# Products of split weights that read the moving tile from the last token to the first, and write the accumulator in the same order

## The chip, the core and the metric

The kernel runs on one core of one Trainium2 chip. The metric is the device time of one launch in microseconds. A core has five instruction streams that matter here: TensorE (PE, with its weight loads listed as PEld), VectorE (DVE), ScalarE (ACT), GpSimd (POOL) and the DMA queues, of which SyncE (SP) issues the weight loads from memory.

## The reference: what is computed

Two blocks of a language model run one after the other over 512 tokens of width 1024, all in float32. The first block projects the normalised input with one matrix `w_in` into four groups of heads (softmax attention with a forget gate, a gated delta rule, two gated linear attentions), projects the result back with `w_out`, and then runs a feed-forward layer with a short convolution (`w_up`, `w_down`, inner width 2816). The second block is a convolution mixer (`conv_w_in`, `conv_w_out`) with a gated feed-forward layer, then latent attention (`w_dkv`, `w_dq`, `w_ukv`, `w_uq`, `w_o`) with another feed-forward layer and a final norm. Cut to what matters here:

```
x = x + token_mix(rms_norm(x), w_in) @ w_out
x = x + conv_glu_ffn(rms_norm(x), w_up, w_down)
h = h + short_conv_mixer(rms_norm_2(h), conv_w_in, conv_w_out)
h = h + swiglu_ffn(rms_norm_2(h), w13, w2)
h = h + mla_mixer(rms_norm_2(h), w_dq, w_uq, w_o, shared_kv(h))
h = h + swiglu_ffn(rms_norm_2(h), w13, w2)
```

Nearly all arithmetic is in the products with the weight matrices. Each has all 512 tokens on one side.

## The kernel before, in words

Activations are kept transposed: features on the 128 partitions, the 512 tokens along the free axis, one tile for each 128 features (`xT`, eight tiles). Weights come in **units**: 128 output columns of a matrix with up to eight blocks of 128 input rows. SP loads a unit into one of four `raw` buffers. ACT copies it into `whi` with rounding to the format fp32r (line 358), and DVE subtracts to get the remainder `wlo` (line 366). There are two `whi` and two `wlo` buffers. Activations are split in the same way into a high and a low tile (`xhi`, `xlo`; `h_hi`, `h_lo` for feed-forward products; `c_hi`, `c_lo` and `chi`, `clo`, `lhi`, `llo` elsewhere).

The function `product` multiplies one unit with the 512 tokens. For each block of input rows it calls `passes`, which issues three matmuls into the same accumulator: high weight with high activation (line 371), high with low (372), low with high (373). The weight is the stationary side (128 x 128), the activation tile the moving side (128 x 512, fp32r), and the output is one whole PSUM bank (128 x 512, float32). `acc(tile)` alternates between two banks. With eight blocks, a unit is a chain of 24 matmuls that add into one bank. The last of the chain carries the semaphore increment (`unit_used` or a named step) that its readers wait for: the evacuation by DVE or ACT out of the bank (line 621 in the up-projections, line 543 in the residuals), and the split of a later unit, which needs the freed `whi` and `wlo`. No reader looks at part of a bank before the chain has ended.

One more place calls `passes` directly (line 2004): the values of the latent attention, where the activation is the stationary side and the weight unit the moving one. The kernel's other matmuls (transposes, the delta rule's triangles and chunks, attention scores) are float32 and do not go through `passes`.

The order of the work on each engine is written out by hand, with hardware loops for the repeated units. PE starts a product when its unit's low half is ready and the bank has been read.

Of the kernel before, what the change touches and what calls it, by code (L numbers as in the profile page):

```python
# [180 lines left out]
class Steps:  # L181
# [8 lines left out]
    def step(self, engine, name):  # L190
        assert name not in self.at, name
        self.count[engine] += 1
        self.at[name] = (engine, self.count[engine])
        return self.sems[engine], 1
# [43 lines left out]
def build(nc, A, cst_d, out_d, known):  # L238
    ctx = ExitStack()
    with ctx:  # L240
# [25 lines left out]
        def acc(tile):  # L266
            return ps[:, tile % 2, :]
# [46 lines left out]
        def unit_view(buf, u):  # L314
            _, kt, n, _ = UNITS[u]
            return buf[:, u % (RAW if buf is raw else PARTS), 0:kt * n].rearrange("p (k c) -> p k c", c=n)
# [4 lines left out]
        def in_loop(value, i, per):  # L321
            return value if i is None else value + per * i
# [46 lines left out]
        def passes(out, wh, wl, xh, xl, first, last):  # L369

            t_.matmul(out, wh, xh, start=first, stop=False)  # L371
            t_.matmul(out, wh, xl, start=False, stop=False)  # L372
            return t_.matmul(out, wl, xh, start=False, stop=last)  # L373

        def product(pe, u, tile, i=None, per=0, x=(xhi, xlo), k0=0, start=True, stop=True, ready=None, cols=0,
                    full=None, order=None, ks=None, reads=False):


            kt = UNITS[u][1]
            pe.wait_ge(lo_split, in_loop(u + 1, i, per))  # L380
            for n, k in list(enumerate(order or range(kt)))[slice(*(ks or (0, kt)))]:
                if ready is not None:
                    ready(pe, k0 + k)
                wh, wl = (unit_view(b, u)[:, k, cols:cols + P] for b in (whi, wlo))
                last = passes(acc(tile), wh, wl, x[0][:, k0 + k, :], x[1][:, k0 + k, :],
                              start and n == 0, stop and n == kt - 1)
                if reads and n < kt - 1:
                    last.then_inc(x_read, 1)
            if ks is None or ks[1] == kt:
                last.then_inc(*(step("pe", full) if full else (unit_used, 1)))  # L390
# [86 lines left out]
        def pe_residual(pe, stage, thirds, x, ready, order=None):  # L477

            per, np_, tiles = round_of(thirds)
            parts = THIRDS if thirds else ((0, KT),)  # L480
            n0 = TILE0[stage]
            regained = x[0] is xhi

            def body(i, last, begin=0):
                for j in range(begin, per):
                    m, part = divmod(j, np_)
                    reads = last and j == per - 1
                    if part == 0:
                        pe.wait_ge(acc_free, n0 + m + 1 + tiles * i)
                    product(pe, FIRST[stage] + j, m, i, per, x, parts[part][0], part == 0, part == np_ - 1,  # L490
                            ready if m == 0 else None, order=None if reads else order, reads=reads)
            if x[0] is c_hi:
                for m, ks in ((0, (0, KT - 1)), (1, (0, KT // 2)), (0, (KT - 1, KT)), (1, (KT // 2, KT))):
                    if ks[0] == 0:
                        pe.wait_ge(acc_free, n0 + m + 1)
                    product(pe, FIRST[stage] + m, m, x=x, ready=ready if m == 0 else None, ks=ks)
                body(0, False, 2)
            with pe.Fori(x[0] is c_hi, KT // tiles - regained) as i:
                body(i, False)
            if regained:  # L500
                body(KT // tiles - 1, True)
# [70 lines left out]
        def pe_up(pe, stage, name, gain, residual):  # L572
            n0 = TILE0[stage]

            def body(i, first):
                for j in range(4):
                    pe.wait_ge(acc_free, n0 + j + 1 + 4 * i)
                    product(pe, FIRST[stage] + j, j, i, 4, ready=parts_of(gain) if first and j == 0 else None)
                    if first and j == 0:
                        pe_sum(pe, name, NORM0[residual])  # L580
            body(0, True)
            with pe.Fori(1, FT // 2) as i:
                body(i, False)
# [2014 lines left out]
```

## Time and profile before

| | |
|---|---|
| median of two runs | 1940.74 us (1940.49 to 1941.0) |
| span of the profiled execution | 1938.3 us |
| median less span | 2.4 us |
| PE busy | 1890.5 us, 98% of the span, 9271 matmul records |
| PEld, DVE, ACT, POOL busy | 1540.8, 959.2, 739.5, 237.1 us |
| mean granted TensorE clock | 0.986 of full speed |
| memory traffic | 161 MB, 83 GB/s |

The span is the time from the first to the last instruction that the hardware profiler recorded in one execution. It has no separately measured time of its own beside it; the span with the 2.4 us by which the median exceeds it is what the sums in this document are made against. Matmuls overlap in the records: one lasts 389 ns by its record while the next has started after some 226 ns. So the sum of durations is more than the busy time, and what a matmul costs in a chain is read from one start to the next. A float32 matmul of the program leaves two records, an fp32r matmul one.

### The profile page before, as it was taken

What the parts mean: (1) busy time and instruction counts of PE and PEld (TensorE: products, weight loads), DVE (VectorE), ACT (ScalarE), POOL (GpSimd) and SP (SyncE); (2) the same over time, 40 slices, a digit from 0 to 9 for tenths busy, and PEclk for the clock granted to TensorE, in tenths of its full rate; (3) what the DMA queues carried; (4) which work ended last, traced back from release to release, by engine and by line L of the source; (5) the groups of instructions that cost most, each with busy time, mean ns of one, the idle gap of its engine ahead of it and who ended that gap; (6) DMA issues with size and microseconds to landing.
All of it is one profiled execution on the core that took longest, in us unless ns stands there. A gap on an engine that the chain in (4) does not pass through costs nothing.

```text
span 1938.3 us, 25963 instructions
## 1 busy us (share of the span) xinstructions
PE 1890.5 (98%) x9271; PEld 1540.8 (79%) x9271; DVE 959.2 (49%) x1354; ACT 739.5 (38%) x1075; POOL 237.1 (12%) x196
## 2 busy tenths in 40 slices
PE   8989999999999999999999999999999999999998
PEld 6778867667888888888888888888776778888887
DVE  6464466654777763344454444333647444444322
ACT  6542543554444443232253333232455343333222
POOL 0051000102111111000021111101000121111100
PEclk9999998999999999999999999999999999999999
DMA  6310211113333333333333333333320133333332
GB/s 193 87 33 1 55 34 34 34 47 89 103 97 97 94 94 94 98 98 98 98 88 104 94 95 97 92 99 101 92 83 22 44 95 94 94 96 96 100 90 73
DMA packets 309223, 161.34 MB, mean 83 GB/s; under 512 B 12688, under 2 KB 306832, under 8 KB 309024
## 3 DMA queue, kind: packets, MB, share of 16 engines
q1 hardware_dynamic: 308080, 157.67, 28.1%
q0 software_dynamic: 640, 2.17, 0.3%
q8 instruction: 48, 0.79, 0.2%
q10 hardware_dynamic: 432, 0.52, 0.1%
q14 instruction: 23, 0.19, 0.0%
HBM read 158.24 MB, written 2.10 MB: 83 GB/s over the span
## 4 chain that ended last, share of the span: by engine, by line
PE 91%; DVE 4%; ACT 3%; issue 1%; POOL 0%; DMA 0%; ACTq 0%; DVEq 0%; POOLq 0%
PE ps L371 26%; PE ps L372 26%; PE ps L373 26%; PE ps L1063 1%; PE ps L1743 1%; PE ps L1491 1%; PE ps L1075 1%; PE ps L1501 1%; PE ps L2039 1%; PE ps L2040 1%; PE ps L1734 1%; PE ps L936 1%; ACT whi L358 1%; PE ps L920 1%; PE ps L1455 0%
## 5 line engine op out<-in xcount | busy, mean ns | idle before, releaser
L371 PE MATMUL ps<-xhi,whi 128*128 128x512 f32 x1656 | 656.6, 396 | 3.1 <-ACT ecol L989 2.1
L372 PE MATMUL ps<-xlo,whi 128*128 128x512 f32 x1656 | 647.7, 391 | 0.0
L373 PE MATMUL ps<-xhi,wlo 128*128 128x512 f32 x1656 | 647.6, 391 | 0.0
L358 ACT ACTIVATE whi<-raw 128x1024 fp32r<-128x1024 f32 (+2 forms) x297 | 309.0, 1040 | 707.6 <-PE ps L373 707.0
L366 DVE TENSOR_TENSOR wlo<-raw,whi 128x1024 fp32r<-128x1024 f32 (+2 forms) x297 | 365.8, 1232 | 278.6 <-ACT whi L358 278.6
L371 PEld LDWEIGHTS ps<-xhi,whi 128*128 128x128 f32 x1656 | 313.1, 189 | 72.1 <-issue 7.9
L373 PEld LDWEIGHTS ps<-xhi,wlo 128*128 128x128 f32 x1656 | 312.8, 189 | 65.9
L372 PEld LDWEIGHTS ps<-xlo,whi 128*128 128x128 f32 x1656 | 313.1, 189 | 65.3 <-issue 2.2
L621 DVE TENSOR_TENSOR zS<-ps,rs 128x512 f32<-128x512 f32 x132 | 91.3, 692 | 296.8 <-PE ps L373 284.6
L373 PE MATMUL ps<-h_hi,wlo 128*128 128x512 f32 x528 | 205.4, 389 | 0.0
L371 PE MATMUL ps<-h_hi,whi 128*128 128x512 f32 x528 | 205.4, 389 | 0.0
L372 PE MATMUL ps<-h_lo,whi 128*128 128x512 f32 x528 | 205.4, 389 | 0.0
L646 POOL TENSOR_TENSOR h_lo<-xg,h_hi 128x512 f32 x66 | 84.9, 1286 | 639.8 <-ACT h_hi L607 639.8
L562 POOL TENSOR_TENSOR ssq<-ssq,sq 128x512 f32<-128x512 f32 x48 | 78.6, 1638 | 555.9 <-ACT sq L510 555.9
L372 PEld LDWEIGHTS ps<-h_lo,whi 128*128 128x128 f32 x528 | 99.1, 188 | 20.7
L373 PEld LDWEIGHTS ps<-h_hi,wlo 128*128 128x128 f32 x528 | 99.1, 188 | 20.6
L371 PEld LDWEIGHTS ps<-h_hi,whi 128*128 128x128 f32 x528 | 99.1, 188 | 20.4
L607 ACT ACTIVATE h_hi<-xg 128x512 f32 x66 | 41.7, 632 | 144.7 <-DVE xg L637 144.7
L543 DVE TENSOR_TENSOR xT<-ps,xT 128x512 f32<-128x512 f32 (+1 forms) x48 | 33.2, 691 | 119.9 <-PE ps L373 119.9
L445 DVE SCALAR_TENSOR_TENSOR xlo<-xT,pcol,xhi 128x512 fp32r<-128x512 f32 (+1 forms) x48 | 47.1, 1009 | 12.6 <-ACT xhi L439 12.6
L439 ACT ACTIVATE xhi<-xT,pcol 128x512 fp32r<-128x512 f32 (+1 forms) x48 | 32.8, 717 | 4.4 <-DVE xT L543 1.0
L510 ACT ACTIVATE sq<-xT 128x512 f32<-128x512 f32 (+1 forms) x48 | 30.1, 626 | 11.1 <-DVE xT L543 10.3
(339 smaller groups left out, 1718.7 us busy)
## 6 DMA issues: line engine op xcount, KB each, us to landing
raw<-in_conv_ffn_w SPq DMA_DIRECT2D x52, 512.0 KB, 3.8
raw<-in_mla_ffn_w SPq DMA_DIRECT2D x52, 512.0 KB, 3.8
raw<-in_w_up SPq DMA_DIRECT2D x44, 512.0 KB, 3.8
raw<-in_w_in SPq DMA_DIRECT2D x28, 512.0 KB, 3.8
raw<-in_conv_w_in SPq DMA_DIRECT2D x24, 512.0 KB, 3.7
raw<-in_w_down SPq DMA_DIRECT2D x16, 448.0 KB, 3.5
raw<-in_conv_ffn_w SPq DMA_DIRECT2D x16, 448.0 KB, 3.5
raw<-in_mla_ffn_w SPq DMA_DIRECT2D x16, 448.0 KB, 3.4
```

The lines of the kernel that those rows point to most:

```text
L358: a.activation(whi[:, u % PARTS, 0:n], raw[:, u % RAW, 0:n], ACT.Copy).then_inc(hi_split, 1)
L366: e.tensor_tensor(wlo[:, u % PARTS, 0:n], raw[:, u % RAW, 0:n], f32(whi[:, u % PARTS, 0:n]), ALU.subtract).then_inc(lo_split, 1)
L371: t_.matmul(out, wh, xh, start=first, stop=False)
L372: t_.matmul(out, wh, xl, start=False, stop=False)
L373: return t_.matmul(out, wl, xh, start=False, stop=last)
L439: a.activation(tile_of(xT if name == "final_norm_g_2" else xhi, k), tile_of(xT, k), ACT.Copy, scale=gain_of(name, k)).then_inc(x_hi, 1)
L445: v.scalar_tensor_tensor(tile_of(xlo, k), tile_of(xT, k), gain_of(name, k), f32(tile_of(xhi, k)), ALU.mult, ALU.subtract).then_inc(x_lo, 1)
L543: v.tensor_tensor(x, acc(m), x, ALU.add).then_inc(acc_free, 1)
L562: g.tensor_tensor(ssq[:, :], ssq[:, :], sq[:, m, :], ALU.add).then_inc(summed, 1)
L607: a.activation(tile_of(h_hi, m), xg[:, pair, :], ACT.Copy).then_inc(prod_hi, 1)
L621: v.tensor_tensor(z, acc(j), rs[:, :], ALU.mult).then_inc(acc_free, 1)
L646: g.tensor_tensor(tile_of(h_lo, m + 2 * i), xg[:, m, :], f32(tile_of(h_hi, m + 2 * i)), ALU.subtract).then_inc(prod_lo, 1)
```

## The change

`product` hands `passes` the accumulator and both activation tiles with the free axis turned round: the first column that is streamed is token 511, the last is token 0, and column by column the output goes to the same token's place as before. The stationary side (`wh`, `wl`), the order of the matmuls, the semaphores, the buffers and everything on other engines are as they were. On every engine the order of the instructions is the same in both kernels (4042 on PE as written, loops not unrolled). The call of `passes` at line 2004 is not changed.

```
--- before.py
+++ after.py
@@ -382,7 +382,7 @@
                 if ready is not None:
                     ready(pe, k0 + k)
                 wh, wl = (unit_view(b, u)[:, k, cols:cols + P] for b in (whi, wlo))
-                last = passes(acc(tile), wh, wl, x[0][:, k0 + k, :], x[1][:, k0 + k, :],
+                last = passes(acc(tile)[:, ::-1], wh, wl, x[0][:, k0 + k, ::-1], x[1][:, k0 + k, ::-1],
                               start and n == 0, stop and n == kt - 1)
                 if reads and n < kt - 1:
                     last.then_inc(x_read, 1)
```

## Rows read from the trace of the kernel before

**Rows 1.** The page: busy time by engine, then the chain of waits.
```profile
PE 1890.5 (98%) x9271; PEld 1540.8 (79%) x9271; DVE 959.2 (49%) x1354; ACT 739.5 (38%) x1075; POOL 237.1 (12%) x196
PE 91%; DVE 4%; ACT 3%; issue 1%; POOL 0%; DMA 0%; ACTq 0%; DVEq 0%; POOLq 0%
```

**Rows 2.** Groups by shape on PE: line, out<-moving,stationary, count | busy us, mean ns | idle before.
```profile
L371 PE MATMUL ps<-xhi,whi 128*128 128x512 f32 x1656 | 656.6, 396 | 3.1 <-ACT ecol L989 2.1 <-DVE xlo L829 1.0
L371 PE MATMUL ps<-h_hi,whi 128*128 128x512 f32 x528 | 205.4, 389 | 0.0
L371 PE MATMUL ps<-c_hi,whi 128*128 128x512 f32 x64 | 24.9, 390 | 0.0
L371 PE MATMUL ps<-chi,whi 128*128 128x512 f32 x36 | 14.9, 415 | 0.3 <-ACT qp L2088 0.3
L371 PE MATMUL ps<-lhi,whi 128*128 128x512 f32 x16 | 7.0, 440 | 0.0
L371 PE MATMUL ps<-whi,lhi 128*128 128x512 f32 x16 | 6.4, 401 | 1.4 <-ACT vtok L2075 1.4
```

**Rows 3.** Busy time by stretch (us from the start): records in brackets, then PE's clock.
```profile
300.00:400.00 100.00, 92.87 (x691) 69.17 (x690) 65.46 (x137) 49.08 (x85) 13.75 (x12) 0.89 0.15 48
600.00:700.00 100.00, 100.00 (x443) 82.81 (x442) 70.06 (x83) 41.59 (x54) 11.62 (x9) 1.00 0.33 97
700.00:800.00 100.00, 100.00 (x443) 82.81 (x442) 40.72 (x41) 31.19 (x37) 10.35 (x8) 1.00 0.32 94
1700.00:1800.00 100.00, 100.00 (x443) 82.83 (x442) 40.18 (x46) 30.12 (x37) 12.43 (x10) 1.00 0.33 96
```

**Rows 4.** PE in order of time, in an up-projection: start us, duration us.
```profile
700.08 0.39 PE L371 MATMUL ps<-xhi,whi 128*128 128x512 f32 x1
700.30 0.39 PE L372 MATMUL ps<-xlo,whi 128*128 128x512 f32 x1
700.53 0.39 PE L373 MATMUL ps<-xhi,wlo 128*128 128x512 f32 x1
700.76 0.39 PE L371 MATMUL ps<-xhi,whi 128*128 128x512 f32 x1
```

**Rows 5.** Who waited for the last matmul of a chain (line 373): us, times.
```profile
  ACT whi L358: 707.0, 219
  DVE zS L621: 284.6, 127
  DVE xT L543: 119.9, 45
```

**Rows 6.** PE in order of time, attention scores in float32 (two records each).
```profile
1459.35 1.02 PE L2039 MATMUL ps<-kn,qn 128*128 128x512 f32 x2
1460.21 1.02 PE L2040 MATMUL ps<-kpz,qp 128*128 128x512 f32 x2
1461.49 0.30 PE L1734 MATMUL ps<-cst,mla_P 128*128 128x128 f32 x1 [0.26 <-DVE mla_P L1794]
```

**Rows 7.** PE in order of time: line 1075, moving runs of 2, then of 32.
```profile
131.93 3.69 PE L1075 MATMUL ps<-mx 128*128 128x64 f32 x32
...
167.32 3.68 PE L1075 MATMUL ps<-mx 128*128 128x64 f32 x32
```

**Rows 8.** Groups on DVE by shape: a scan forward (1517), a scan backward (1519).
```profile
L1517 DVE TENSOR_TENSOR_SCAN mx<-mx 128x512 f32<-128x512 f32 x3 | 3.6, 1216 | 0.0
L1519 DVE TENSOR_TENSOR_SCAN mx<-mx,lastone 128x512 f32<-128x512 f32 x3 | 3.6, 1197 | 0.0
```

More of the change, by code:

```diff
@@ L384, in product @@
                 wh, wl = (unit_view(b, u)[:, k, cols:cols + P] for b in (whi, wlo))
-                last = passes(acc(tile), wh, wl, x[0][:, k0 + k, :], x[1][:, k0 + k, :],
+                last = passes(acc(tile)[:, ::-1], wh, wl, x[0][:, k0 + k, ::-1], x[1][:, k0 + k, ::-1],
                               start and n == 0, stop and n == kt - 1)
```

## The prediction

> **What bounds the kernel now.** I read the page's first part and its chain of waits first. PE is busy for 1890.5 us of 1938.3 and holds 91% of the chain; DVE, at 959.2 us, is the next engine and has half of that [rows 1]. So the time is PE's, and the question is which of PE's work the change touches. The groups by shape say that [rows 2]: line 371 ran 1656 + 528 + 64 + 36 + 16 = 2300 times with an activation tile as the moving side, and lines 372 and 373 as often, which makes 6900 matmuls that get a reversed moving tile and a reversed output. The last row of the group, 16 of each line with `whi` moving, is the direct call of `passes` and stays as it was: 48 matmuls.
>
> What one of them costs is not its duration (389 ns) but the distance between starts. The windows show 443 records in each 100 us of three stretches that hold nothing but products, with the clock at 1.00 (the upper of the two levels, 2.4 GHz) and PE busy 100.00 us: 100/443 = 225.7 ns for one [rows 3]. The timeline shows the same from near: 700.08 to 700.76 for three, 227 ns each, with no gap at line 373, the end of a triple [rows 4]. So the products take 6900 x 0.2257 = 1557 us, 80% of the span. The other 381 us are float32 matmuls and stages where DVE and ACT are waited for; there the clock falls too (0.89 between 300 and 400 us) [rows 3].
>
> The readers of a bank wait for the chain's last matmul and for nothing before it: 707.0 us of ACT's idle time and 284.6 and 119.9 us of DVE's end there [rows 5]. That idle time is slack of engines off the path. It also says that the direction in which a bank is filled is seen by no reader: when the last matmul ends, all of the bank is there, in either direction.
>
> **The change part by part.**
>
> Instructions: none is added, taken away or moved, on any engine. The cost of issue and of the semaphores is 0. No wait goes and none comes, so nothing is late next as long as a matmul takes as long as before. If one took longer, PE would still be the bound, since DVE is idle for half of the time and the DMA engines are busy for a third (0.33) [rows 1, 3].
>
> The one term is therefore 6900 x d, where d is what the reversed direction adds to the 225.7 ns of one product matmul. No matmul of the kernel before has a negative step, on the moving side or on the output, so d is bounded by the nearest rows.
>
> The upper bound is the rate at which this kernel's float32 matmuls take 512 columns. Two records of line 2039 start at 1459.35 and line 2040 follows at 1460.21, so one record, a stream of 512 columns, takes 430 ns [rows 6]. That is what a product costs if a column needs a whole slot for itself in place of sharing one with its neighbour: d = 430 - 225.7 = 204.3 ns, or 6900 x 0.2043 = 1410 us.
>
> The lower bound comes from the same rows. Half of 430 is 215, so the product's 225.7 has 10.7 ns in it beyond the column stream at twice that rate. If something in the seam between two matmuls of a chain costs those 10.7 ns and the reversed order avoided it, d = -10.7 ns and the term is -74 us.
>
> What row is nearest? Two bear on it. VectorE has a scan over 512 elements that reads and writes with step -1, in float32, just behind a forward one of the same shape: 1197 ns against 1216, so reading and writing SBUF backwards costs this engine nothing [rows 8]. It is another engine and at 2.3 ns an element a much slower one, so it says little about a stream at 0.44 ns a column. On PE itself, line 1075 reads its moving side in runs of 2 columns (every other pair) at 131.93 and in runs of 32 at 167.32: 3.69 and 3.68 us for 32 records, 115 ns a record in both [rows 7]. Broken runs of moving columns cost nothing that shows. This is weaker than it looks, because 64 columns at 430/512 ns are 54 ns, and so anything up to twice that is hidden in the 115 ns.
>
> I take d = 0. The streamed columns have the same addresses and the same neighbours in memory as before, and so have the output columns; only the order within a pair turns. The distance between two additions to one column stays 512 columns, since all matmuls of a chain run the same way. The seams between a reversed chain and a forward matmul are few (a chain of 24 runs between them), and even at 10.7 ns for each of some 297 units they are 3 us.
>
> The row on runs of two [rows 7] reads the moving side only; its output is written straight on. On the output the Trainium skill has a rule against this change: its page "Advanced Engine Details and Errata", section "Memory Cachelines", says that PSUM works in lines of two float32 values and that every two consecutive elements should be contiguous, or matmuls slow down significantly. If a falling step counts as not contiguous, the page leads to the half-rate case below; if what counts is that both columns lie in one line, it leads to my forecast. No run so far shows which.
>
> The sum: span 1938.3 + 6900 x 0 = 1938.3 us, and with the 2.4 us by which the median lies above the span, 1941 us, the median of before.
>
> **The rivals.**
>
> *Half rate.* Each pair of columns is no longer taken together, on the way in from SBUF or on the way out to PSUM, and a product matmul takes as long as a float32 record, 430 ns. The place is every product chain; the cost is +1410 us, so 3350 us. It decides as soon as the pairing works for rising addresses alone, and a tenth of its price would already be 141 us. Stages where PE waits now could take up at most its idle time, 1938.3 - 1890.5 = 48 us, so between 3300 and 3350 us. For it speaks that a product gets its 512 float32-wide columns through at 512/225.7 = 2.27 columns a nanosecond, nearly twice the rate of the float32 records [rows 4, 6]: something there handles more than one column at a time, and such a thing may have a direction. Against it speaks that a backward stream costs VectorE nothing [rows 8].
>
> *A dearer seam.* The stream keeps its rate, but each reversed matmul starts with the upper end of a line and pays once more what the seam costs now, 10.7 ns. 6900 x 10.7 ns = +74 us: 2015 us, slower by 3.8%. It needs only 5.6 ns a matmul (39 us in all) to pass 2%. Rows 4 show that matmul follows matmul without any slack for it.
>
> *A cheaper seam.* The 10.7 ns are lost between two matmuls in a way that depends on the direction, and go: 1941 - 74 = 1867 us. The Trainium skill's page "TensorE: Matmul & The Clock Gate", section "Back-to-back issue gap", gives N/2.4 + 2.5 ns, 216 ns for 512 columns, where this trace has 225.7; it says nothing of a direction. What stands against this is that nothing in the trace ties the extra time to the order of the columns; the records of the weight load (442 in 100 us, 82.8 us busy) are as good a candidate, and they don't change [rows 3].
>
> *The change does nothing at all*, because the direction is lost on the way to the chip, gives the forecast's number too.
>
> **How the numbers follow.** The forecast with d = 0 (and the direction that is lost) gets 0.68: one scan and one pattern of short runs, both clean, and no consumer that could see the difference. Half rate gets 0.18: its mechanism is plain, and the product's 0.44 ns a column is a rate that no backward row of the trace has been seen at. The dearer seam gets 0.11, the cheaper 0.03. The time is the likeliest one, 1941 us. By itself the forecast would lie within 1936 to 1946. The range has to hold 8 in 10, so it takes in the dearer seam at the top, 2015 us; on the low side the cheaper seam is too unlikely to be needed, and 1935 closes the range, which holds 0.68 + 0.11 = 0.79, with small seam gains in it about 0.8. The half rate stays outside. About 2% is what a measurement of this kernel can tell from no change, and that gives: faster 0.03, within 2% 0.69 (a seam dearer by under 5.6 ns is in it), slower 0.28.
>
> **What would show it.** In the profile after, the stretch from 700 to 800 us should again hold 443 records at clock 1.00 and three matmuls of a unit should start 0.23 us apart with durations of 389 ns. Busy times of DVE, ACT and POOL should be the same to a microsecond or two. With half rate the window would hold some 232 records, line 371's mean would rise from 389 to about 590 ns, and the idle time of ACT and DVE behind line 373 would about double. With the dearer seam there would be 423 records. If the time rose with the windows at 443, the cause would lie in the other 381 us, which I hold untouched; if the rise differed between chains with `xhi` and with `h_hi` as the moving tile, it would lie in the buffers' places and not in the direction.

## The result, and the profile after

The changed kernel takes 1983.75 us in the median (1983.6 to 1983.9) against 1940.74 before: a ratio of 1.0231, with a 95% interval from 1.0192 to 1.027. It is slower by 43 us. That it is slower is clear; that it is slower by more than 2% is not, from these two executions on each side. The time lies in the stated range. The likeliest case, no change, did not come. What came has the form of the rival named "a dearer seam", a fixed addition to each matmul, at 58% of its price.

The page of the changed kernel, busy time by engine and then the chain of waits, answers to [rows 1]:

```profile
PE 1935.9 (98%) x9271; PEld 1546.2 (78%) x9271; DVE 953.8 (48%) x1354; ACT 740.6 (37%) x1075; POOL 235.9 (12%) x196
PE 92%; DVE 4%; ACT 2%; issue 1%; POOL 0%; DMA 0%; ACTq 0%; DVEq 0%; POOLq 0%
```

PE is busy 45.4 us longer (1935.9 against 1890.5), with the same number of records; the span grew by 43.5 us (1981.8 against 1938.3). So all of it lies in PE's own work, and PE's waits even shrank by 2 us. Nothing else moved by more than 6 us.

The windows of the changed kernel (records in brackets, the clock in the third column from the right) answer to [rows 3]:

```profile
600.00:700.00 100.00, 100.00 (x431) 80.71 (x430) 66.96 (x81) 41.68 (x54) 11.53 (x9) 1.00 0.32 94
700.00:800.00 100.00, 100.00 (x430) 80.77 (x429) 42.94 (x46) 32.15 (x39) 10.13 (x8) 1.00 0.31 92
1700.00:1800.00 100.00, 100.00 (x430) 80.72 (x430) 39.92 (x45) 29.45 (x36) 11.49 (x9) 1.00 0.31 92
```

There are 430 to 431 records where 443 stood, at the same clock and with PE as full as before. Such a count takes in the one or two records that began before the window, so dividing 100 us by it gives a distance that is about 1 ns too short. Starts that lie far apart give the distance itself. These are starts of line 371, first one of the kernel before, then two of the changed kernel:

```profile
500.16 0.39 PE L371 MATMUL ps<-xhi,whi 128*128 128x512 f32 x1
```

```profile
500.45 0.40 PE L371 MATMUL ps<-xhi,whi 128*128 128x512 f32 x1
699.96 0.40 PE L371 MATMUL ps<-xhi,whi 128*128 128x512 f32 x1
```

In the kernel before, 294 triples (a triple is the three matmuls of one call of `passes`) lie between 500.16 and 700.08 us [rows 4]: 680.0 ns a triple, 226.7 ns a matmul. In the changed kernel 285 triples lie between the two starts: 700.0 and 233.3 ns. That is 6.7 ns more for each product matmul, and 6900 x 6.7 ns = 46 us. It accounts for PE's 45.4 us.

The profile holds a control inside the same run. These are rows of line 373 of the changed kernel, durations in ns as smallest, median, largest:

```profile
L373 PE MATMUL ps<-h_hi,wlo x528: 397/398/398, 722.8 to 1968.9; 128*128 128x512 f32 x176
L373 PE MATMUL ps<-c_hi,wlo x64: 397/398/398, 981.3 to 1025.4; 128*128 128x512 f32 x64
L373 PE MATMUL ps<-chi,wlo x36: 395/398/398, 1460.2 to 1488.6; 128*128 128x512 f32 x36
L373 PE MATMUL ps<-lhi,wlo x16: 397/398/399, 1433.6 to 1446.7; 128*128 128x512 f32 x16
L373 PE MATMUL ps<-whi,llo x16: 388/389/390, 1447.4 to 1459.5; 128*128 128x512 f32 x16
```

Each of these buffers that is read backward shows 398 ns in the median, where it had 389 before, and with hardly any spread. The last row is the direct call of `passes`, which still reads forward: it stayed at 389, between neighbours in time that did not (`lhi`, until 1446.7 us, and `chi`, from 1460.2 us). So the cost follows the direction, and neither the buffer nor the stage. The recorded duration rose by 9 ns and the distance between starts by 6.7; since matmuls overlap in the records, the distance is what counts.

### The profile page after: what moved, and what is told of

It reads as the page before. It is cut to its first block, busy times and chain, and to the rows that moved or that the text cites. A ratio compares the mean times of both kernels' runs of the same rounds, so it can differ in the third digit from the quotient of the medians.

```text
span 1981.8 us, 25963 instructions
## 1 busy us (share of the span) xinstructions
PE 1935.9 (98%) x9271; PEld 1546.2 (78%) x9271; DVE 953.8 (48%) x1354; ACT 740.6 (37%) x1075; POOL 235.9 (12%) x196
## 4 chain that ended last, share of the span: by engine, by line
PE 92%; DVE 4%; ACT 2%; issue 1%; POOL 0%; DMA 0%; ACTq 0%; DVEq 0%; POOLq 0%
PE ps L371 27%; PE ps L373 27%; PE ps L372 27%; PE ps L1063 1%; PE ps L1743 1%; PE ps L1491 1%; PE ps L1075 1%; PE ps L2039 1%; PE ps L2040 1%; PE ps L1501 1%; PE ps L1734 1%; PE ps L920 1%; PE ps L936 1%; PE ps L1455 1%; DVE xlo L445 0%
## 5 line engine op out<-in xcount | busy, mean ns | idle before, releaser
L371 PE MATMUL ps<-xhi,whi 128*128 128x512 f32 x1656 | 670.9, 405 | 3.2 <-DVE wlo L366 2.1
L372 PE MATMUL ps<-xlo,whi 128*128 128x512 f32 x1656 | 662.3, 400 | 0.0
L373 PE MATMUL ps<-xhi,wlo 128*128 128x512 f32 x1656 | 661.8, 400 | 0.0
L358 ACT ACTIVATE whi<-raw 128x1024 fp32r<-128x1024 f32 (+2 forms) x297 | 308.8, 1040 | 745.3 <-PE ps L373 743.7
L366 DVE TENSOR_TENSOR wlo<-raw,whi 128x1024 fp32r<-128x1024 f32 (+2 forms) x297 | 360.7, 1215 | 286.7 <-ACT whi L358 286.6
L621 DVE TENSOR_TENSOR zS<-ps,rs 128x512 f32<-128x512 f32 x132 | 91.3, 692 | 321.2 <-PE ps L373 308.9
L373 PE MATMUL ps<-h_hi,wlo 128*128 128x512 f32 x528 | 210.0, 398 | 0.0
L371 PE MATMUL ps<-h_hi,whi 128*128 128x512 f32 x528 | 209.9, 398 | 0.0
L372 PE MATMUL ps<-h_lo,whi 128*128 128x512 f32 x528 | 209.9, 398 | 0.0
```

The source lines that it names most:

```text
L358: a.activation(whi[:, u % PARTS, 0:n], raw[:, u % RAW, 0:n], ACT.Copy).then_inc(hi_split, 1)
L366: e.tensor_tensor(wlo[:, u % PARTS, 0:n], raw[:, u % RAW, 0:n], f32(whi[:, u % PARTS, 0:n]), ALU.subtract).then_inc(lo_split, 1)
L621: v.tensor_tensor(z, acc(j), rs[:, :], ALU.mult).then_inc(acc_free, 1)
```

## The experiments

Two questions were open. The first is the side: theory R puts the cost where the moving tile is read, theory W where the accumulator is written. The second is the form: for either side, the cost can be fixed for each matmul (theory F, the seam) or gather by the column or by the step down (theory L). Twelve kernels were run, the first two timed in three rounds, the rest with one profile each. In the profiles I read the number of records in 100 us of pure products, as above, and where single nanoseconds matter the distance of starts between 500 and 700 us. The kernel before took between 1935.3 us (mean clock 0.990) and 1942.3 us (0.985) in 13 executions beside the one-sided kernels, so a difference of under 7 us between two single executions says nothing by itself.

### One side alone

```
-                last = passes(acc(tile), wh, wl, x[0][:, k0 + k, :], x[1][:, k0 + k, :],
+                last = passes(acc(tile), wh, wl, x[0][:, k0 + k, ::-1], x[1][:, k0 + k, ::-1],
```

> Only the moving side of the products runs backward; the output is written forward, so each accumulator holds its tokens in the wrong order and the result is not the reference's. Theory R (the extra time arises where the moving tile is read from SBUF): 1984 us, 430 records in 100 us of a product stretch, as with both reversed. Theory W (it arises where the accumulator is written): 1941 us, 443 records. If both sides contribute: between the two, and the other one-sided kernel has the rest.

```
-                last = passes(acc(tile), wh, wl, x[0][:, k0 + k, :], x[1][:, k0 + k, :],
+                last = passes(acc(tile)[:, ::-1], wh, wl, x[0][:, k0 + k, :], x[1][:, k0 + k, :],
```

> Only the output of the products runs backward; the moving side is read forward, so the tokens stand in the wrong order and the result is not the reference's. Theory W (writing the accumulator backward costs the time): 1984 us, 430 records in 100 us. Theory R (reading backward costs it): 1941 us, 443 records.

Moving side alone: 1984.05 us, ratio 1.0232 (1.0215 to 1.0249) to the kernel before on the same chip. Output alone: 1940.03 us, ratio 0.9994 (0.9983 to 1.0006). The windows agree; first the kernel that reads backward, then the one that writes backward:

```profile
600.00:700.00 100.00, 100.00 (x430) 80.59 (x429) 67.36 (x81) 42.05 (x54) 11.54 (x9) 1.00 0.32 93
700.00:800.00 100.00, 100.00 (x431) 80.55 (x430) 42.63 (x45) 31.76 (x39) 10.14 (x8) 1.00 0.32 92
```

```profile
600.00:700.00 100.00, 100.00 (x443) 82.84 (x442) 71.13 (x83) 42.12 (x55) 11.95 (x10) 1.00 0.32 94
700.00:800.00 100.00, 100.00 (x443) 82.84 (x442) 41.14 (x42) 31.19 (x37) 10.34 (x8) 1.00 0.33 97
```

This settles the side. All of the cost is in reading the moving tile; writing float32 columns to PSUM in falling order costs nothing, to within two tenths of a per cent (0.9983 to 1.0006). Theory W is out, and with it, for a falling step, the Trainium skill's rule of the page "Advanced Engine Details and Errata", section "Memory Cachelines", that I had weighed against the change: adjacent columns in falling order were as good as in rising order here.

### One matmul of three backward

```
-            t_.matmul(out, wh, xl, start=False, stop=False)
+            t_.matmul(out[:, ::-1], wh, xl[:, ::-1], start=False, stop=False)
```

> Of the three matmuls of a triple only the middle one runs backward, moving side and output both; the other two forward. If the cost belongs to each reversed matmul (6.3 ns by 43 us / 6900): a third of it, 1955 us, some 439 records in 100 us. If it belongs to a chain in which every matmul starts at the upper end, or to the turn from one direction to the other: 1941 us in the first case; in the second, two turns in each triple, well over 1955 us, since the column written last is then the one that the next matmul adds to first.

It took 1954.96 us, 439 records in 100 us. The groups by shape of this kernel (mean ns behind the busy time) show where:

```profile
L372 PE MATMUL ps<-h_lo,whi 128*128 128x512 f32 x528 | 209.1, 396 | 0.0
L373 PE MATMUL ps<-h_hi,wlo 128*128 128x512 f32 x528 | 205.9, 390 | 0.0
L371 PE MATMUL ps<-h_hi,whi 128*128 128x512 f32 x528 | 205.4, 389 | 0.0
```

By their starts, three matmuls take 686.7 ns against 680.0 before: 6.7 ns more for one backward matmul among forward ones, a third of the change's 20 ns. The cost belongs to the backward matmul itself (line 372, 396 ns), and a turn of direction between two matmuls adds nothing, though the next one then adds first to the column that was written last. The edit also turned the middle matmul of the direct call, 16 in all, which is 0.1 us.

### How fine must the falling order be?

In these four kernels both sides go down in blocks and forward within a block; the block has b columns.

```
+        def down(ap):
+
+            return ap.rearrange("p (n b) -> p n b", b=2)[:, ::-1, :]
...
-                last = passes(acc(tile), wh, wl, x[0][:, k0 + k, :], x[1][:, k0 + k, :],
+                last = passes(down(acc(tile)), wh, wl, down(x[0][:, k0 + k, :]), down(x[1][:, k0 + k, :]),
```

With b = 2:

> Both sides run through pairs of columns: the last pair first, within a pair forward (steps -2 and 1). If the falling order inside a pair is what costs: 1941 us. If going down from line to line or starting at the top costs: 1984 us. If a pattern of two dimensions has a price of its own or breaks the pairing: more than 1984 us.

With b = 4:

> As the run with pairs, but in blocks of four columns (16 bytes of a partition): the last block first, within a block forward, on both sides. If the cost comes from leaving or entering a 16-byte line at the wrong end: 1941 us. If it comes from going down through memory at all, or from starting near the top of the tile: 1984 us.

With b = 256:

> Both sides run forward in two blocks of 256 columns, the upper block first: one step down in each matmul. If any step down costs a fixed time: 1984 us. If starting away from the tile's first column costs it: 1984 us too. If the cost gathers over many small steps down, or lies in a start that is not on a larger boundary: 1941 us.

With b = 16:

> Both sides in blocks of 16 columns, the last block first, within a block forward: 31 steps down in a matmul, where blocks of four have 127 and the full cost. Theory F (a fixed cost of a matmul that goes down, whatever the number of steps): 1984 us, 430 records in 100 us. Theory L (each step down costs a little, 6.5 ns / 127): 6900 x 1.6 ns = 11 us more than before, 1952 us, 440 records.

With b = 64:

> The same in blocks of 64 columns: 7 steps down. Theory F: 1984 us, 430 records. Theory L: 6900 x 0.36 ns = 2.5 us more, 1943 us, 442 to 443 records. If the cost is only there when the first step down comes within some number of columns from the start: 1941 us here and 1984 us with 16, or 1941 us with both.

| block | steps down | us | records, 600 to 700 us |
|---|---|---|---|
| 1 (the change) | 511 | 1983.75 | 431 |
| 2 | 255 | 1983.07 | 430 |
| 4 | 127 | 1985.5 | 431 |
| 16 | 31 | 1983.8 | 431 |
| 64 | 7 | 1938.41 | 443 |
| 256 | 1 | 1942.15 | 443 |
| 512 (before) | 0 | 1940.74 | 443 |

The windows of the kernels with blocks of 16 and of 64, in that order:

```profile
600.00:700.00 100.00, 100.00 (x431) 80.55 (x430) 67.28 (x81) 41.86 (x54) 11.66 (x9) 1.00 0.32 93
```

```profile
600.00:700.00 100.00, 100.00 (x443) 82.81 (x442) 70.11 (x83) 43.04 (x56) 11.62 (x9) 1.00 0.33 97
```

It is a step and not a slope. From 31 to 511 steps down the cost is the same (700.0 ns a triple in the blocks of 4 and of 16 as in the changed kernel), and at 7 it is gone (680.0 ns). Theory L wanted 440 records with blocks of 16 and got 431, so the cost does not gather by the step. Theory F as I had put it wanted 430 with blocks of 64 and got 443, so it isn't enough to start high in the tile and go down some time. The third reading on record fits: a fixed cost that appears when the read turns down early in the matmul, after 16 columns or fewer but not after 64. It isn't the only one that fits, since four things change together with the block:

- the place of the first step down;
- the number of steps, where the limit would lie between 7 and 31;
- the bytes that a step passes over (a step down goes from the end of one block to the start of the one below);
- the start address. A start away from the first column is no explanation as such, since the run with blocks of 256 starts at column 256 and the one with 64 at column 448, both at no cost. But all kernels of the table that pay start at column 496 or above, and none was run that starts there and then reads forward, so a cost of starting near the tile's end, or off some larger boundary, is not excluded.

These runs don't part the four.

### Does the cost grow with the columns?

Two pairs of kernels were meant to ask that directly. In the first, the middle matmul is cut in two, forward as the control and then backward:

```
-            t_.matmul(out, wh, xl, start=False, stop=False)
+            for c in (slice(0, T // 2), slice(T // 2, T)):
+                t_.matmul(out[:, c], wh, xl[:, c], start=False, stop=False)
```

> The middle matmul of each triple is cut into two of 256 columns, all forward: the control for the next run. 2316 matmuls more, each with a seam of about 10.7 ns: 1941 + 25 = 1966 us, and more if the weight load of 128 columns no longer hides behind 256 columns.

```
-            t_.matmul(out, wh, xl, start=False, stop=False)
+            for c in (slice(0, T // 2), slice(T // 2, T)):
+                t_.matmul(out[:, c][:, ::-1], wh, xl[:, c][:, ::-1], start=False, stop=False)
```

> The same cut, both halves of the middle matmul backward. Seam theory (a fixed cost at each backward matmul, 6.3 ns): 2 x 2316 x 6.3 ns = 29 us above the control with forward halves. Stream theory (each column a little slower, 6.3 ns over 512): 14.5 us above it, as with one uncut backward matmul in the middle.

1979.86 us forward and 1984.78 backward. The windows, forward first, with four records to a group in place of three:

```profile
600.00:700.00 100.00, 100.00 (x576) 87.27 (x575) 67.71 (x81) 42.35 (x54) 11.70 (x9) 1.00 0.33 94
```

```profile
600.00:700.00 100.00, 100.00 (x574) 87.32 (x573) 67.68 (x81) 42.32 (x54) 11.68 (x9) 1.00 0.32 93
```

By its starts, a group takes 696.7 ns forward, 16.7 above the uncut 680.0, where I had expected 10.7. Backward it takes 700.0, only 3.3 ns more for two backward matmuls. Seam and stream theory wanted 29 and 14.5 us. 4.9 came, and 2300 x 3.3 ns = 7.7 us would be due by the starts; single executions don't part these two, and the forward one ran at a mean clock of 0.983 against 0.985. Both missed, in opposite company: the control was dearer than expected by 14 us (1979.86 against 1966), and the backward version hardly dearer than the control.

In the second pair the last two matmuls of a triple are shortened to 384 columns:

```
-            t_.matmul(out, wh, xl, start=False, stop=False)
-            return t_.matmul(out, wl, xh, start=False, stop=last)
+            c = slice(0, 384)
+            t_.matmul(out[:, c], wh, xl[:, c], start=False, stop=False)
+            return t_.matmul(out[:, c], wl, xh[:, c], start=False, stop=last)
```

> The second and third matmul of each triple take only the first 384 of the 512 columns, so the low parts are left out for the last 128 tokens. All forward: the control. 4632 x 128/2.4 = 247 us less than before: 1694 us. Durations of lines 373 and 374 389 - 53 = 336 ns.

The backward version puts `[:, ::-1]` behind each `[:, c]`.

> The same short matmuls, these two backward on both sides (columns 383 to 0), the low parts for the last 128 tokens left out again. Theory F (fixed cost, 6.3 to 6.7 ns for each): 4632 x 6.5 = 30 us above the control. Theory L or any cost by the column: three quarters of it, 23 us above the control.

1740.45 us forward (1694 was expected) and 1728.84 backward: the backward one is 12 us **faster**. Neither theory allows that sign. The windows, forward first:

```profile
600.00:700.00 100.00, 100.00 (x513) 92.89 (x513) 67.28 (x76) 44.10 (x57) 13.11 (x12) 1.00 0.38 110
```

```profile
600.00:700.00 100.00, 100.00 (x519) 93.32 (x518) 67.83 (x77) 44.42 (x56) 13.89 (x12) 1.00 0.38 110
```

And two of the groups by shape, forward and then backward (the third, line 373, has 338 ns in both):

```profile
L371 PE MATMUL ps<-h_hi,whi 128*128 128x512 f32 x528 | 205.9, 390 | 0.0
L374 PE MATMUL ps<-h_hi,wlo 128*128 128x384 f32 x528 | 180.8, 342 | 0.0
```

```profile
L371 PE MATMUL ps<-h_hi,whi 128*128 128x512 f32 x528 | 204.9, 388 | 0.0
L374 PE MATMUL ps<-h_hi,wlo 128*128 128x384 f32 x528 | 180.6, 342 | 0.0
```

By its starts, a triple takes 586.7 ns forward and 580.0 backward, a difference of 6.7 ns, the same size as that of one backward matmul but of the other sign. The control again is the surprise. A triple less 256 columns, at the 215 ns for 512 that half a float32 record gives [rows 6], should take 680.0 - 107.5 = 572.5 ns. Forward it is 14 ns above that, backward 7.5.

What follows is smaller than I wanted and still useful. In the two mixes of lengths that were run, forward matmuls cost more than their columns explain, and turning the short ones round took 6.7 ns off the triple. So the 6.7 ns are no property of a backward stream as such, and whether they would grow with the columns was not answered: neither pair came out as either theory wanted. All distances found, for triples with 512 columns throughout (680.0, 686.7, 700.0 ns), with halves (696.7, 700.0) and shortened (580.0, 586.7), lie whole multiples of 3.3 ns apart, which is 8 cycles at the clock's upper level of 2.4 GHz. That looks like waiting in portions between one matmul and the next, which is a guess from the sizes. One idea is that it depends on what the weight load reads at the same time; no run here tests it. Another is that it depends on where the read before ended. In chains of 512 columns the run with one backward matmul speaks against it: a backward matmul pays 6.7 ns behind a forward one as behind a backward one, and a forward one behind a backward one pays nothing. The cause at that depth stays open.

## Why the prediction was right or wrong

**What bounds the kernel, and how many matmuls are touched: right.** PE held the whole change. The count of 6900 times the measured 6.7 ns gives 46 us against the 45.4 us by which PE's busy time grew, and the 48 untouched matmuls stayed at 389 ns.

**The distance of starts: read 1 ns too short.** The 225.7 ns came from the count of records in a window; the starts give 226.7. So the products took 6900 x 226.7 ns = 1564 us and not 1557, and the seam had 11.7 ns beyond half a float32 record and not 10.7. The conclusions don't hang on it.

**Nothing else moves: right.** No wait came or went beyond PE's own pace. ACT's idle time behind line 373 rose from 707.0 us [rows 5] to 743.7, DVE's at line 621 from 284.6 to 308.9, which is the slower PE seen from its readers:

```profile
  ACT whi L358: 743.7, 227
  DVE zS L621: 308.9, 128
  DVE xT L543: 126.9, 45
```

**The term d: wrong in the value chosen.** This is the step that failed. I took d = 0; it is 6.7 ns. I leaned on two rows. The backward scan of VectorE [rows 8] is another engine with its own read, and told nothing about TensorE's. The runs of two columns on PE [rows 7] lay under a floor of 110 ns a record and could not have shown 6.7 ns in a stream that I had put at 54 (32 records of 64 columns took 3.53 us, from 131.93 to the next start at 135.46, and 128 columns at 1456.75 us took 110 ns a record as well); I had said as much, and then let the row count all the same. Both rows were clean because they could not be otherwise. They excluded a large cost in the one case and none at all in the other, and what they left open was exactly a small fixed cost on each of 6900 matmuls, at 7 us a nanosecond.

**The dearer seam: right in kind, oversized.** The rival priced the seam's second payment at the 10.7 ns that the present seam costs, 74 us in all. Measured are 6.7 ns and 43 us. That its cost doesn't go with the number of steps down is shown by the blocks of 1 to 16, all at 430 or 431 records; that it is the same for matmuls of other lengths is not shown. Its mechanism as I wrote it, "starts with the upper end of a line", is wrong for lines of up to 64 bytes: blocks of 4 and of 16 columns, 16 and 64 bytes of a partition, start at the lower end of their block and pay the same. The price had no other ground than the size of the present seam, so that the measured one fell below it, and with it into the range, was luck in the size.

**The half rate: wrong**, and the fear behind it with it. A matmul of 512 columns takes 233.3 ns in falling order and not 430, and the output side shows no cost at all. The argument for this rival was unsound too: 226.7 ns are 544 cycles at the 2.4 GHz of clock 1.00, more than one for each of the 512 columns, so nothing in the rows asked for columns to be taken in pairs.

**The chances.** 0.68 for d = 0 against 0.11 for the rival that came was too sure, given that 39 us of 1941 were enough to pass 2% and the term had a factor of 6900 in it. The range, drawn to take in the dearer seam, held the time (1983.75 within 1935 to 2015), while the sum itself missed.

## What to carry to other kernels

Where one instruction form makes up most of the bound engine's chain, multiply its count by one nanosecond first (here 7 us): any edit of its access patterns is then a bet on single nanoseconds, and a row that hides a few of them under another floor is no evidence. Count records in a window that holds nothing else, before and after; 443 against 430 shows some 7 ns for each of thousands of matmuls in a single profile, and the distance between two far starts, divided by the matmuls between them, gives it to a tenth. In chains of 512-column matmuls leave the moving tile in rising order, while the output's order is free: a reversed output alone cost nothing, and neither did blocks of 64 or 256 columns in falling order on both sides (one execution each).

## What the runs showed of the hardware that was not expected

- TensorE reading an fp32r moving tile of 512 columns in falling order costs 6.7 ns a matmul (226.7 to 233.3 ns from start to start); writing PSUM in falling order costs nothing (ratio 0.9994, 0.9983 to 1.0006).
- The cost is all or nothing: the same in falling blocks of 1, 2, 4 and 16 columns, absent in blocks of 64 and 256.
- Cutting one of three 512-column matmuls into two of 256 adds 16.7 ns to the triple (680.0 to 696.7), and shortening two of three to 384 columns saves 93 ns (680.0 to 586.7) where the columns alone would give 107.5. The seam between matmuls is not one number; over the kernels run here it moves in portions of 3.3 ns with lengths and directions, and once (384 columns) in favour of the backward read.
